# Expert blocks of a mixture-of-experts layer: gate and up in one 256-column product, the weight slot carried in a register, and the transpose of the product rows as four column-tiled identity products

## What is computed

```python
def moe(x2, w_router, router_bias, w1, w3, w2):
    expert_idx, gate_w = route(x2, w_router, router_bias)   # 2 of 16 experts per token
    ...
    def run_block(args):
        e, toks = args
        xb = x_pad[toks]
        h = jax.nn.silu(xb @ w1[e]) * (xb @ w3[e])
        return h @ w2[e]
    yb = lax.map(run_block, (blk_e, slot_tok.reshape(n_blk, MOE_BLOCK)))
    y = yb.reshape(-1, D) * slot_gate[:, None]
    return jnp.zeros((N + 1, D), x2.dtype).at[slot_tok].add(y)[:N]
```

## Time and profile before

| | us |
|---|---|
| median of 3 runs | 3313.47 |
| lowest, highest | 3309.04, 3322.31 |
| span of the profiled execution, which is also its own time | 3333.5 |
| PE busy | 3119.7 (94%) |
| DVE busy | 1931.1 (58%) |
| ACT busy | 873.4 (26%) |

### The profile page before, as it was taken

One profiled execution on the slowest core, in us unless ns is written; L12 is line 12 of the kernel. 1 busy time (PEld: TensorE's weight loads), 2 busy tenths in 40 slices (PEclk: granted clock), 3 DMA queues, 4 the chain that ended last, 5 costly groups with the idle time before them and its releaser, 6 DMA issues.

```text
span 3333.5 us, 73560 instructions
## 1 busy us (share of the span) xinstructions
PE 3119.7 (94%) x28638; PEld 2349.2 (70%) x28639; DVE 1931.1 (58%) x3792; ACT 873.4 (26%) x1559; POOL 422.1 (13%) x345
## 2 busy tenths in 40 slices
PE   8998999799988998999699979999999899999997
PEld 5445887577765445886577748888778578588886
DVE  1476574456641575664555657664576656476644
ACT  1116110356632116110456641000022522110000
POOL 1000000322222000000322210000055133000000
PEclk9999999899999999999899989999999999999998
DMA  7110323389952110323389942222334000122231
GB/s 284 63 64 1 127 89 146 126 322 377 380 215 92 52 62 14 127 89 152 124 334 375 375 158 86 89 89 89 103 96 107 25 2 3 62 79 87 89 99 66
DMA packets 83202, 443.23 MB, mean 133 GB/s; under 512 B 19480, under 2 KB 19616, under 8 KB 39336
## 3 DMA queue, kind: packets, MB, share of 16 engines
q1 hardware_dynamic: 56488, 381.70, 31.5%
q0 software_dynamic: 23568, 55.62, 4.6%
q10 hardware_dynamic: 2928, 3.07, 0.3%
HBM read 411.00 MB, written 29.23 MB: 132 GB/s over the span
## 4 chain that ended last, share of the span: by engine, by line
PE 88%; ACT 4%; issue 4%; DVE 3%; DVEq 1%; DMA 0%; POOL 0%; ACTq 0%; POOLq 0%
PE pb L1223 24%; PE pb L788 12%; PE pb L1094 11%; PE pb L955 9%; PE pb L1117 5%; PE pb L995 4%; PE pb L1337 4%; PE pb L1049 3%; PE pb L1604 2%; ACT arena L1632 1%; PE pb L824 1%; PE pb L892 1%; PE pb L935 1%; PE pb L1101 1%; ACT xT L1662 1%
## 5 line engine op out<-in xcount | busy, mean ns | idle before, releaser
L1223 PE MATMUL pb<-arena,streamed 128*128 128x256 f32 x1952 | 446.6, 381 | 3.6 <-DVE arena L2496 2.8
L1223 PEld LDWEIGHTS pb<-arena,streamed 128*128 128x128 f32 x1952 | 372.6, 191 | 56.8 <-ACT xT L1662 3.2
L1094 PE MATMUL pb<-streamed,xT 128*32 128x128 f32 x9024 | 358.9, 276 | 11.5 <-issue 11.3
L1094 PE MATMUL pb<-arena,xT 128*32 x3008 | 353.3, 276 | 16.1 <-issue 10.2
L788 PE MATMUL pb<-xT,streamed 128*128 128x512 f32 x832 | 367.8, 600 | 0.0
L1094 PEld LDWEIGHTS pb<-arena,xT 128*32 128x32 f32 x3008 | 322.9, 111 | 30.6 <-issue 24.5
L1094 PEld LDWEIGHTS pb<-streamed,xT 128*32 128x32 f32 x9024 | 327.9, 111 | 15.9 <-issue 15.8
L788 PEld LDWEIGHTS pb<-xT,streamed 128*128 128x128 f32 x832 | 159.4, 193 | 200.9 <-issue 200.8
L1758 ACT ACTIVATE streamed<-arena 128x3072 f32 x94 | 260.2, 2768 | 56.1 <-remote 37.5
L1223 PE MATMUL pb<-arena,am 128*128 128x256 f32 x976 | 227.3, 379 | 0.0
L1117 PE MATMUL pb<-arena,am 128*32 x3008 | 193.7, 391 | 23.4 <-issue 18.5
(11 more groups left out here) (497 smaller groups left out, 5393.0 us busy)
## 6 DMA issues: line engine op xcount, KB each, us to landing
arena<-in_w_moe SPq DMA_DIRECT2D x192, 1024.0 KB, 9.6
streamed<-in_w_tail SPq DMA_DIRECT2D x87, 1024.0 KB, 5.0
streamed<-in_w_layer SPq DMA_DIRECT2D x78, 1024.0 KB, 4.9
xT<-xs_dram POOLq DMA_DIRECT2D x22, 512.0 KB, 8.4
ys_dram<-xT POOLq DMA_DIRECT2D x88, 128.0 KB, 9.1
xs_dram<-lnw POOLq DMA_DIRECT2D x12, 512.0 KB, 18.8
arena<-rel_dram SPq DMA_DIRECT2D x8, 448.0 KB, 9.4
lnw<-in_ln_par POOLq DMA_DIRECT2D x3, 1024.0 KB, 6.8
```

Of the source, the lines that this page charges most:

```text
L1094: last = mm(pb[m][r0:r0 + MOE_BLOCK, 0:FW], rows, w, start=(k == 0), stop=(k == KC - 1))
L1223: last = mm(pb[p][:, 0:HALF], stat(i), mov(i), start=(opens and i == 0), stop=(closes and i == steps - 1))
```

## The change

In each block, `up` takes gate and up columns together: a moving operand of two runs of 128 columns, one from w1 and one from w3, and one PSUM bank whose columns 0 to 127 are gate and 128 to 255 up. The outer loop is no longer w1, then w3, but the first half of the width (k = 0 to 3), then the second (k = 4 to 7). Pieces, relays and semaphores go by those halves: DVE relays the front half of both matrices (`relay_front`), now ahead of `hidden`, and ACT the back half (`relay_back`). `gate_half` waits for the second `up_ready` instead of the first. `turn` is four column-tiled products with the identity as the moving operand. In s = 1 the slot of block b - 1 comes from a register that is written at the end of the loop body.

```diff
+        PARTS = ((0, 2), (1, 3), (4, 5))
+        def part_of(p):
+            return p % 2 if p < UP_PIECES else 2
+        def both(at, k):
+            return arena[:, bass.ds(at + k * D_EXP, UP_PIECES * PAIR)].rearrange("p (m n) -> p m n", m=2)
+        def of_expert(at, first):
+            w = arena[:, bass.ds(at, UP_PIECES * PAIR)].rearrange("p (m k c) -> p m k c", m=2, k=KC)
+            return w[:, :, first:first + KC // 2, FW:D_EXP]
...
-        w1_relay, w3_relay = streamed[:, 0:RELAY], streamed[:, RELAY:2 * RELAY]
+        up_relay = streamed[:, 0:2 * RELAY].rearrange("p (m k c) -> p m k c", m=2, k=KC)
...
                 if s < 2:
-                    sp.wait_ge(up_ready, 2 * layers * N_BLK + 1 + s)
+                    sp.wait_ge(up_ready, 2 * layers * N_BLK + 2)
...
-                        load(e, 2 * m)
-                        load(e, 2 * m + 1)
+                        for p in PARTS[m]:
+                            load(e, p)
...
-                    for m, (relay, relayed) in enumerate(((w1_relay, w1_relayed), (w3_relay, w3_relayed))):
+                    for half, relayed in enumerate((front_relayed, back_relayed)):
                         pe.wait_ge(relayed, l * N_BLK + b + 1)
                         alone(pe)
-                        for k in range(KC):
+                        for k in range(half * KC // 2, (half + 1) * KC // 2):
...
-                                last = mm(pb[m][r0:r0 + MOE_BLOCK, 0:FW], rows, w, start=(k == 0), stop=(k == KC - 1))
+                                w = both(off, k)[:, :, 0:FW] if g == 0 else up_relay[:, :, k, (g - 1) * FW:g * FW]
+                                last = mm(cut(pb[0][r0:r0 + MOE_BLOCK, 0:2 * FW], FW), rows, w, start=(k == 0), stop=(k == KC - 1))
                         last.then_inc(up_ready, 1)
...
                     pe.wait_ge(hid_ready, l * N_BLK + b + 1)
-                    for c in range(FW // P):
-                        last = nc.tensor.transpose(pb[6][:, c * P:(c + 1) * P], hid[:, c * P:(c + 1) * P], identity)
+                    for g in range(COLS):
+                        r0 = g * MOE_BLOCK
+                        last = mm(pb[6][r0:r0 + MOE_BLOCK, 0:FW], hid[:, r0:r0 + MOE_BLOCK], identity, start=True, stop=True)
...
+                pe.reg_mov(slot_before, slot(0))
                 with pe.Fori(0, N_TILE - 1) as i:
+                    off = pe.snap(slot_before, min_val=0, max_val=SLOT)
                     for s in range(1, COLS + 1):
...
-                        if s == 1:
-                            off = slot(b - 1)
...
                         off = ahead
+                    pe.reg_mov(slot_before, ahead)
...
-                    act.wait_ge(expert_here[0], l * N_EXP + e + 1)
+                    act.wait_ge(expert_here[1], l * N_EXP + e + 1)
                     alone(act)
-                    fn(cut(w1_relay, D_EXP - FW), ..., ACT.Copy).then_inc(w1_relayed, 1)
+                    fn(up_relay[:, :, KC // 2:KC], of_expert(slot_of(e), KC // 2), ACT.Copy).then_inc(back_relayed, 1)
...
-                    act.wait_ge(up_ready, 2 * (l * N_BLK + b) + 3)
+                    act.wait_ge(up_ready, 2 * (l * N_BLK + b) + 4)
...
+                def relay_front(b, e):
+                    dve.wait_ge(expert_here[0], l * N_EXP + e + 1)
                     alone(dve)
+                    if b:
+                        dve.wait_ge(up_ready, 2 * (l * N_BLK + b - 1) + 3)
+                        alone(dve)
+                    v.tensor_copy(up_relay[:, :, 0:KC // 2], of_expert(slot_of(e), 0)).then_inc(front_relayed, 1)
...
-                    dve.wait_ge(up_ready, 2 * (l * N_BLK + b) + 4)
-                    alone(dve)
                     dve.wait_ge(sil_ready, l * N_BLK + b + 1)
                     alone(dve)
-                    v.tensor_tensor(hid, pb[1][:, 0:FW], sil, ALU.mult).then_inc(hid_ready, 1)
+                    v.tensor_tensor(hid, pb[0][:, FW:2 * FW], sil, ALU.mult).then_inc(hid_ready, 1)
...
+                    if b + 1 < N_BLK:
+                        relay_front(b + 1, ahead)
                     hidden(b)
...
-                    if b + 1 < N_BLK:
-                        relay_w3(b + 1, ahead)
```

More of the change, by code:

```diff
@@ L343, in two_blocks @@
         xs_loaded = sem("xs_loaded")
-        expert_loaded = [sem(f"expert_loaded_{n}") for n in ("w1", "w3", "w2")]
-        expert_here = [sem(f"expert_here_{n}") for n in ("w1", "w3", "w2")]
-        w1_relayed, w3_relayed, w2_relayed = sem("w1_relayed"), sem("w3_relayed"), sem("w2_relayed")
+        expert_loaded = [sem(f"expert_loaded_{n}") for n in ("front", "back", "down")]
+        expert_here = [sem(f"expert_here_{n}") for n in ("front", "back", "down")]
+        front_relayed, back_relayed, w2_relayed = sem("front_relayed"), sem("back_relayed"), sem("w2_relayed")
         xs_tr, xsT_ready = sem("xs_transposed"), sem("xsT_ready")
@@ L501, in load @@
                     sp.dma_start(piece(e, p), a["w_moe"][bass.ds((l * N_EXP + e) * PIECES + p, 1)]
-                                 .rearrange("a p n -> p (a n)")).then_inc(expert_loaded[p // 2], 16)
+                                 .rearrange("a p n -> p (a n)")).then_inc(expert_loaded[part_of(p)], 16)
                 def arrived(e, m):
@@ L521, in _ @@
                 load(1, 0)
+                arrived(0, 1)
                 load(1, 1)
-                arrived(0, 1)
                 load(1, 2)
@@ L528, in _ @@
                 arrived(0, 2)
-                load(1, 4)
-                load(1, 5)
+                for p in PARTS[2]:
+                    load(1, p)
                 sp.wait_ge(route_ready, l + 1)
@@ L771, in _ @@
             mm = nc.tensor.matmul
+            slot_before = pe.alloc_register("slot_before")
             def pair(j, l=None, i=0, per=1):
@@ L1085, in up @@
                     alone(pe)
-                    for m, (relay, relayed) in enumerate(((w1_relay, w1_relayed), (w3_relay, w3_relayed))):
+                    for half, relayed in enumerate((front_relayed, back_relayed)):
                         pe.wait_ge(relayed, l * N_BLK + b + 1)
                         alone(pe)
-                        for k in range(KC):
+                        for k in range(half * KC // 2, (half + 1) * KC // 2):
+                            rows = xsT[:, k * P + s % COLS * MOE_BLOCK:k * P + (s % COLS + 1) * MOE_BLOCK]
                             for g in range(COLS):
                                 r0 = g * MOE_BLOCK
-                                rows = xsT[:, k * P + s % COLS * MOE_BLOCK:k * P + (s % COLS + 1) * MOE_BLOCK]
-                                w = arena[:, bass.ds(off + (m * KC + k) * D_EXP, FW)] if g == 0 else relay[:, (k * (COLS - 1) + g - 1) * FW:(k * (COLS - 1) + g) * FW]
-                                last = mm(pb[m][r0:r0 + MOE_BLOCK, 0:FW], rows, w, start=(k == 0), stop=(k == KC - 1))
+                                w = both(off, k)[:, :, 0:FW] if g == 0 else up_relay[:, :, k, (g - 1) * FW:g * FW]
+                                last = mm(cut(pb[0][r0:r0 + MOE_BLOCK, 0:2 * FW], FW), rows, w, start=(k == 0), stop=(k == KC - 1))
                         last.then_inc(up_ready, 1)
@@ L1796, in _ @@
                 alone(act)
-                relay_w1(0, block_expert(act, 0))
+                relay_back(0, block_expert(act, 0))
                 fn(primed, ones[:, 0:1], ACT.Silu)
@@ L1804, in _ @@
                     if b + 1 < N_BLK:
-                        relay_w1(b + 1, e)
+                        relay_back(b + 1, e)
                     if b == 0:
@@ L2380, in _ @@
                 e = block_expert(dve, 0)
-                relay_w3(0, e)
+                relay_front(0, e)
                 v.tensor_tensor(r_t, r_pick, r_score, ALU.mult)
```

6 lines of the change are left out of this document (1 added, 5 removed).

## The result

The changed kernel takes 3337.28 us (median of 6 runs, 3334.51 to 3347.09) where the kernel before takes 3317.59 (6 runs, 3309.04 to 3325.76): ratio 1.0071, 95% interval 1.0052 to 1.0089. The first profiled execution of before was not typical: it spans 3333.5 us, and a second one, profiled later (label e0_before_again), 3310.1. I compare with both.

A forecast was written before the change was run, and what follows sets the result against it. TensorE was taken to bound the kernel (88% of the chain), with hidden product and tile copy last afterwards. Full passes +38, first passes and ends +3, ring slot +1, code -15: +27, giving 3340 us, own range 3325 to 3360.

The forecast's parts named there:

- Step 8.48 in s=3 blocks: Up-to-up step where the next tile's xsT copies wait behind ScalarE's later relay: 8.48 us where 6.85 stood, the largest term.
- Steps 5.92 in s=1 and s=2: Up-to-up steps set by the later hidden product and PE's sequencer: 5.92 us where 6.36 and 5.63 stood.
- Step 6.47 at the loop's end: Up-to-up step of the s=4 block, including 0.12 for two register moves: 6.47 us where 6.05 stood.
- VectorE's relay ends "near T + 0.4": Front relay ahead of the hidden product, T being up's end: product at T + 0.58 fits by 0.1 to 0.2, cost zero.
- The second half of up: Its wait for ScalarE's back relay: covered by 0.33 us; without that cover 0.3 a block at most.
- The slot of s=1: Before down in s=1 the 0.72 us second slot load goes; hidden path then last, so 0.44 gained.
- The turn hidden at no cost: PE's turn falls from 0.38 to 0.22 us; the 0.16 gain is hidden because turn is not last.
- Part 6: Stops in code met for the first time shrink with 35% fewer PE instructions: 7 us in first passes, 8 at ends.
- Ring slot: Load for what follows the layer, asked for at the end of the last up, not its middle: 1 us (0 to 4), once.
- A (code gives back more: Code stops in first passes and last blocks fall by 30 us instead of 15: 3315, no change; chance 0.23.
- B (PE last everywhere, then a DMA floor): PE ends last at every up, then DMA share 0.98 binds in the middle: 3266, or 3284 with that limit; chance 0.15.
- C (clock): New idle before s=4 blocks drops PE's clock to 1.2 GHz in half of 20 passes: +17 to +34, 3365; chance 0.12.

The follow-up runs named there:

- e1: The changed kernel with ScalarE's two xsT copies, once in four blocks, issued ahead of its back relay instead of behind it: 3314.7 us, 0.9992 of before.
- e3: The changed kernel with the xsT copies moved from ScalarE to VectorE, behind its hidden product: 3309.0 us, 0.9974 of before.
- b2: The kernel before with only the new turn, four column-tiled products with the identity: 3327.6 us, 1.0022 of before.
- b1: The kernel before with only the slot carried in a register, without the second read in s=1: 3303.7 us, 0.9943 of before.
- e2: The changed kernel with the next block's slot read ahead of the wait for the hidden product and carried across the loop's end: 3325.2 us, 1.0017 of before.
- e4: The changed kernel with both the slot read early and the xsT copies on VectorE: 3282.6 us, 0.9880 of before; repeated, 3285.6 us, 0.9923.
- e5: The changed kernel with early slot read and xsT copies on VectorE, but turn as before's single fp32 transpose: 3284.2 us, 0.9911 of before.
- a1: The changed kernel with two 128-column products in place of each 256-column one for gate and up: 3369.7 us, 1.0138 of before.

## Why the prediction came out right

The forecast was 3340 and slower; the time is 3337.28. The nearness is in part luck. 27 us were added to a median of three runs, 3313.47; the medians of six runs each differ by 19.7. The account, changed kernel less the second profile of before, on blocks 5 to 44: 262.81 and 262.02 less 244.12 and 245.78, +34.9. First five: -5.6 and -2.7. From block 44 to the last down: -2.7 and +1.1. Together +25.0, and with the wait for the ring slot 27; the spans differ by 22.1. Set beside the forecast: full passes +34.9 for +38, first passes -8.3 for -5, last parts -1.6 for -7, ring slot +2.3 for +1. The mechanism and its largest term were right; the sum of the rest came out by errors that cancel. A pass became longer by 1.62, not 1.90, since the pass read for the forecast, 24.89, was 0.17 shorter than the mean of 25.06, and the four new steps together came 0.11 below the forecast 26.79.

**Step 8.48 in s=3 blocks: right.** 8.54. Relay to T + 3.38 (forecast 3.39), copies to T + 4.35 (4.36), up at T + 4.88 (4.84). e1 and e3 show the cause.

**Steps 5.92 in s=1 and s=2: right, 0.05 to 0.08 too high.** 5.87 and 5.84. The hidden product ends at T + 0.86 (0.87), the next up starts 1.32 to 1.35 behind. I took 1.34 and added 0.07 for 14 more instructions; b2 shows that the addition is real with the old order (0.02 to 0.10), in the changed kernel it isn't seen in these two steps.

**Step 6.47 at the loop's end: right.** 6.38, with 1.86 from hid end to up where I took 1.96. The 0.12 for the two register moves came from no row, and no run shows it: b1 has the moves and the same 1.8 as before. b2, with the new turn and without the moves, has 1.89.

**VectorE's relay ends "near T + 0.4", hidden product fits by 0.1 to 0.2: it fits by 0.02.** The relay ends at T + 0.55 and the product starts at T + 0.57. The s=2 step in the pass shown above is one of three in the profile, block 5 aside, where it does not fit, for a reason that the rows leave open: 6.08 in place of 5.84. The relay of the next block there ran to T + 0.9. It does not fit in block 5 of either layer, whose up ends at 691.86 in the first layer (VectorE of the changed kernel, timeline):

```profile
689.24 2.65 DVE L2458 TENSOR_SCALAR xtok<-xtok 128x1024 f32<-128x1024 f32 x4
692.41 1.75 DVE L2397 COPY streamed<-arena 128x3072 f32 x1
694.08 0.28 DVE L2448 TENSOR_TENSOR am<-pb,am 128x128 f32<-128x128 f32 x1
```

The scaling that `scale_residual` does once a layer (L2458) now has the front relay behind it and only then the hidden product, at T + 2.22. The step is 7.52 in both layers where before had 6.6 to 6.9. The forecast had no term for this.

**The second half of up, "0.3 a block at most" without its cover: right.** e2 and e4 took the cover away: 0.20; e1 did once a pass: 0.24.

**The slot of s=1, "a gain of 0.44": right as the share of the sum, not as what the part is worth.** The step went from 6.42 to 5.87. b1 shows 0.72 to 0.76 a pass when nothing else is late. The changed kernel could not keep the rest because its hidden path was late.

**The turn hidden at no cost: half right.** It gains nothing in the changed kernel, costs 0.29 a pass in before (b2), and 0.09 a pass is all it gives even in e4 (e5). In e4 the next up starts 0.19 ahead of the turn's end; with the full-array turn of e5 and before, 0.07. The Trainium skill, TensorEngine Tiling (Array Packing), Key Properties, has a change of tiling mode drain TensorE, and this agrees with it: up and the new turn share a mode.

**Part 6, -15 for code: the sum right, both terms wrong.** -7 for the first passes: the stops fell from 9.2 to 2.7 in each layer (means over both profiles of each kernel), 13 in all, and a1 ties that to the instruction count. -8 for the last parts: nothing of note, since the 10.8 and 13.0 of stops that I divided were 2 and 1 in the second profile. I had read one execution's accident as the kernel's; that 13 and nothing add up near 15 is luck. The Trainium skill, Runtime: NRT & Kernel Launch, Instruction fetch mechanics, has PE hold 2048 instructions. By that figure (an estimate) a body of 1304 or of 848 stays held after its first pass; the traces agree, as the stops that go with the count are in the first passes.

**Ring slot: 1 us forecast, 2.3 measured.** The stretch 973.07:975.40 above is PE waiting for that load in the first layer; in the changed kernel's second profile the distance to the next product is 1.8, in both of before it is zero.

**Rivals.** A (code gives back 30): in the first profile's accounts it seems so, -31 in the four stretches; the second profile shows 18 of it to be chance. B (PE last everywhere, then a DMA floor): it did not happen in the changed kernel, PE was idle 11.5% in the middle; but the floor itself was wrong, as e4 shows. C (clock): it did not happen: the middle's clock is 1.00 with 1.77 idle in each pass. It was slow for 3.3 us in before's first pass behind a stop of 2.20, and what fell away there is part of the first passes' gain.

What stays open: why the last blocks of the first profile stopped; their rows name no releaser, and it came in neither layer of any other profile, so no run could take it apart. Nor does a row show what PE waits for in the stops of a first pass: that they are the loading of code is argued from their going with the instruction count.

## What to carry to other kernels

When a change makes a step later, follow every instruction queued behind it on its engine: here ScalarE's silu moved by 1.7 us, which cost 0.2 to 0.3 a block by itself, while the copies behind the relay behind it cost 1.67 once in four blocks. On an engine that stood idle they cost nothing (e3); first in the queue they still cost 0.3 a pass, in the relay that then comes late (e1). Before pricing a saving from stops that name no releaser, look at a second profile: the stops that come again belong to the kernel. And an edit's price depends on what is last when it is made: the same turn cost 0.29 a pass in before and gave 0.09 in e4, and the carried slot gave 0.76 a pass in before, while the s=1 step of the changed kernel fell by 0.55 in all.

## What the hardware showed that I had not expected

- A DMA share of 0.98 was no floor here. The same loads ran at 377 GB/s with share 0.98 in before and at 394 with share 1.00 in e4; between them the pass became 5% shorter.
- Two 128-column fp32 products in a row on one column tile cost more than the same products with the four tiles in turn: an up of 3.88 against 3.70 us.
- Stops in code met for the first time fell faster than the instruction count: kernels with 1304 instructions of PE a pass have 6.7 to 12.7 us of them in a layer, kernels with 848 have 1.1 to 5.5.
- Reading a word of SBUF into a PE register ahead of a semaphore wait instead of behind it took 0.42 to 0.59 us off the way from the hidden product to the next up (e2), more than the 0.30 of the load itself; the address work behind the load moved with it.
